# First units on x without its norm's factor, half units given out otherwise, bias in four transfers

## The reference

```python
h = _rms(x, norm1_g)                       # x / sqrt(mean(x*x) + eps) * gain
p_rwkv, q, k, v, qm, gates = split(h @ w_in)
o_a = _rwkv(p_rwkv, ...)                   # token recurrence of 8 heads x 64, delta rule, state S
o_b = sliding-window attention(q, k, v)    # 8 query / 2 key heads, ALiBi bias, sink, window 128
o_m = _mem_attend(qm, mk, mv)              # 4 heads x 128 over 256 memory tokens
br = stack([o_a, o_b, o_m]) @ w_branch     # each to 1024
x = x + sum(sigmoid(gates) * br) @ w_out
h = _rms(x, norm2_g)
a_in, u = split(h @ w_up)
x = x + (gelu(conv3(a_in)) * u) @ w_down
```

## Time and profile before

| what | us |
|---|---|
| median of 3 runs | 2136.68 |
| lowest, highest | 2133.88, 2139.18 |
| the profiled execution | 2136.24 |
| its span | 2134.2 |
| TensorE busy in it | 2066.6 |
| VectorE, ScalarE, GpSimd busy | 1264.5, 945.4, 148.0 |

### The profile page before, as it was taken

The page is one execution under the profiler, slowest core; times in us unless marked ns, Lnnn a source line. Parts: engine busy times, 40 slices in busy tenths (PEclk is TensorE's granted clock), DMA queues, the critical chain, the costliest instruction groups (busy, mean ns, idle before and its releaser), DMA issues.

```text
span 2134.2 us, 41128 instructions
## 1 busy us (share of the span) xinstructions
PE 2066.6 (97%) x17305; PEld 1965.7 (92%) x17305; DVE 1264.5 (59%) x2079; ACT 945.4 (44%) x1563; POOL 148.0 (7%) x238
## 2 busy tenths in 40 slices
PE   6999999999999999999999999999999999999999
PEld 5888899899999998889989999999878898899999
DVE  5566653656666545674446666654466645677753
ACT  5566332445444425643333544443375333455442
POOL 1000001001111000001000011100000110011110
PEclk9999999999999998999999999999999999999999
DMA  4422211354445452231124444445423213544544
GB/s 164 141 92 76 69 58 56 94 160 123 126 127 157 141 154 88 71 94 47 56 72 147 126 128 129 129 154 149 143 95 86 76 47 83 159 141 151 152 151 135
DMA packets 98487, 242.63 MB, mean 114 GB/s; under 512 B 24320, under 2 KB 38656, under 8 KB 98304
## 3 DMA queue, kind: packets, MB, share of 16 engines
q1 hardware_dynamic: 98304, 240.01, 37.3%
HBM read 233.88 MB, written 6.09 MB: 112 GB/s over the span
## 4 chain that ended last, share of the span: by engine, by line
PE 86%; DVE 6%; ACT 3%; issue 2%; DMA 1%; SPq 1%; DVEq 0%; ACTq 0%
PE sums L300 24%; PE sums L302 22%; PE sums L301 22%; PE px L1491 5%; DVE w_lo L476 1%; PE px L1504 1%; PE ps_t L1019 1%; PE ps_o L1041 1%; PE pz L1767 1%; PE ps_x L969 1%; PE ps_s L1005 1%; PE ps_o L1036 1%; ACT w_hi L318 1%; PE ps_s L1002 1%; DVE s L1120 1%
## 5 line engine op out<-in xcount | busy, mean ns | idle before, releaser
L300 PE MATMUL sums<-x_hi,w_hi 128*128 128x384 f32 (+1 forms) x2208 | 741.7, 336 | 22.2 <-DVE q L498 8.4
L302 PE MATMUL sums<-x_hi,w_lo 128*128 128x384 f32 (+1 forms) x2208 | 724.0, 328 | 0.0
L301 PE MATMUL sums<-x_lo,w_hi 128*128 128x384 f32 (+1 forms) x2208 | 723.8, 328 | 0.0
L476 DVE TENSOR_TENSOR w_lo<-raw,w_hi 128x1024 fp32r<-128x1024 f32 (+2 forms) x449 | 524.2, 1168 | 302.8 <-ACT w_hi L318 302.3
L318 ACT ACTIVATE w_hi<-raw 128x1024 fp32r<-128x1024 f32 (+1 forms) x452 | 441.0, 976 | 500.8 <-PE sums L302 279.5
L300 PEld LDWEIGHTS sums<-x_hi,w_hi 128*128 128x128 f32 x2208 | 417.7, 189 | 45.4 <-issue 29.8
L301 PEld LDWEIGHTS sums<-x_lo,w_hi 128*128 128x128 f32 x2208 | 418.4, 190 | 1.4
L302 PEld LDWEIGHTS sums<-x_hi,w_lo 128*128 128x128 f32 x2208 | 417.6, 189 | 0.0
L300 PE MATMUL sums<-h_hi,w_hi 128*128 128x384 f32 (+1 forms) x528 | 172.5, 327 | 0.0
L302 PE MATMUL sums<-h_hi,w_lo 128*128 128x384 f32 (+1 forms) x528 | 172.0, 326 | 0.0
L301 PE MATMUL sums<-h_lo,w_hi 128*128 128x384 f32 (+1 forms) x528 | 172.0, 326 | 0.0
(11 more groups left out here) (302 smaller groups left out, 2500.3 us busy)
## 6 DMA issues: line engine op xcount, KB each, us to landing
raw<-w_up SPq DMA_DIRECT2D x132, 512.0 KB, 3.6
raw<-w_gate SPq DMA_DIRECT2D x72, 512.0 KB, 3.6
raw<-w_down SPq DMA_DIRECT2D x48, 512.0 KB, 3.7
raw<-w_rwkv SPq DMA_DIRECT2D x42, 512.0 KB, 3.6
raw<-w_branch SPq DMA_DIRECT2D x72, 256.0 KB, 2.7
raw<-w_attn SPq DMA_DIRECT2D x30, 512.0 KB, 3.7
raw<-w_out SPq DMA_DIRECT2D x24, 512.0 KB, 3.6
raw<-w_down_end SPq DMA_DIRECT2D x24, 384.0 KB, 3.1
```

What stands on the lines that cost most here:

```text
L300: pe.matmul(out, wh[:, ws], n.hi[:, k, :], start=(n.begins and k == 0), stop=False)
L301: pe.matmul(out, wh[:, ws], n.lo[:, k, :], start=False, stop=False)
L302: mm = pe.matmul(out, wl[:, ws], n.hi[:, k, :], start=False, stop=(n.ends and k == n.kt - 1))
L476: dve.tensor_tensor(lo_of(c, u), raw_of(c, u), hi_of(c, u).bitcast(F32), ALU.subtract).then_inc(S["w_lo_dve"], 1)
```

## The change

Five edits, none of which adds or removes a matmul.

1. **Start.** Norm 0 is replaced by `first_*`, ten steps that hold units 0 and 1 among them (halves after each step: 0, 0, 1, 0, 2, 1, 0, 0, 0, 0, then one more). Units 0 and 1 (k and v of group 0) take `g_hi`, `g_lo`, the two parts of x times gain, and their sums are multiplied by the norm's factor `n1_y` when they are evacuated. Squares wait for x alone; `ones` is loaded behind the first part of x, `vecs` behind all of x. Unit 0 is split by VectorE, units 1 and 2 by GpSimd. The constants' loads and copies come behind unit 0's release of its weight tile. Norm 1 is woven with 12 halves instead of 14, and as `m_hi` lies on `g_hi`, it waits for units 0 and 1.
2. **Bias.** Four transfers of four heads each, two in the first step of `keys_sync` and two in the second, instead of eight of two heads in the first.
3. **Attention.** The 29 halves are 2, 2, 2 and then 23 spread over 20 steps. Before, they were spread over all 23.
4. **Recurrence.** The 48 halves have 3, 2 behind the preparation and then 26 over the rest of the scan; before 2 and then 29.
5. **Stores.** In the last group the tables are issued first, the state's stores three and four steps later.

```diff
-            unit("pa", g, m, T, a["w_attn"][m], DT, c.x_hi[:, :, x], c.x_lo[:, :, x],
-                 splitter="pool" if g == 0 and n < 3 else "dve", needs=ready if n == 0 else None)
+            if g == 0 and n < FIRST_UNITS:
+                unit("pa", g, m, T, a["w_attn"][m], DT, c.g_hi[:, :, x], c.g_lo[:, :, x],
+                     splitter="pool" if n else "dve", needs=gained if n == 0 else None)
+            else:
+                unit("pa", g, m, T, a["w_attn"][m], DT, c.x_hi[:, :, x], c.x_lo[:, :, x],
+                     splitter="pool" if g == 0 and n == 2 else "dve", needs=ready if n in (0, FIRST_UNITS) else None)
...
+        if n.kind == "pa" and m in (4, 5) and g == 0:
+            dve.wait_ge(S["n1_y"], ROOT)
+            dve.tensor_tensor((c.k_raw if m == 4 else c.vw)[:, 0:T], bank(c, n), c.n1_y[:, 0:T], ALU.mult).then_inc(free, 1)
...
+def first_act(act, c):
...
+    def rounded(k):
+        act.activation(c.g_hi[:, k, col], w.buf[:, k, :], ACT.Identity, scale=vec(c, w.gain, k)).then_inc(S["g_hi"], 1)
+
+    yield
+    for k in range(0, DT, 2):
+        act.wait_ge(S[f"x_in{k // 2}"], 16)
+        act.activation(c.first_sq[:, k, col], w.buf[:, k, :], ACT.Square).then_inc(S["even_sq"], 1)
+    yield
+    act.wait_ge(S["vecs_in"], 16)
+    for k in (0, 1):
+        rounded(k)
+    yield
+    for k in range(2, DT):
+        rounded(k)
+    yield
+    rsqrt_act(act, c, c.n1_xs[:, col], c.n1_t[:, col], c.n1_y[:, col], S["n1_y"], 1)
+    yield
+    for k in range(DT):
+        act.wait_ge(S["x_normed"], k + 1)
+        act.activation(w.hi[:, k, :], w.buf[:, k, :], ACT.Copy).then_inc(S["x_hi_done"], 1)
...
+def first_dve(dve, c):
...
+    def rest(k):
+        dve.wait_ge(S["g_hi"], k + 1)
+        dve.scalar_tensor_tensor(c.g_lo[:, k, col], w.buf[:, k, :], vec(c, w.gain, k), c.g_hi[:, k, col].bitcast(F32),
+                                 ALU.mult, ALU.subtract).then_inc(S["g_lo"], 1)
+
+    yield
+    for k in range(1, DT, 2):
+        dve.wait_ge(S[f"x_in{k // 2}"], 16)
+        dve.tensor_tensor(c.first_sq[:, k, col], w.buf[:, k, :], w.buf[:, k, :], ALU.mult).then_inc(S["odd_sq"], 1)
+    yield
+    dve.wait_ge(S["vecs_in"], 16)
+    for k in (0, 1):
+        rest(k)
+    yield
+    for k in (2, 3):
+        rest(k)
+    dve.wait_ge(S["n1_mean"], 1)
+    dve.tensor_scalar(c.n1_xs[:, col], c.ps_n[:, col], 1.0 / D, RMS_EPS, ALU.mult, ALU.add).then_inc(S["n1_y"], 1)
+    for k in range(4, DT):
+        rest(k)
+    yield
+    rsqrt_dve(dve, c.n1_xs[:, col], c.n1_t[:, col], c.n1_y[:, col], S["n1_y"], 1)
...
+    def bias(e):
+        for u in range(2):
+            sp.dma_start(c.bias[H[u], e, :, u * CHUNK:u * CHUNK + KEYS], c.a["alibi"][H[e], 2, :, :]).then_inc(S["bias_in"], 16)
...
-    for e in range(2):
-        for u in range(2):
-            for r in range(2):
-                sp.dma_start(c.bias[H[u], r, e, :, u * CHUNK:u * CHUNK + KEYS],
-                             c.a["alibi"][H[e], 2, 2 * r:2 * r + 2, :]).then_inc(S["bias_in"], 16)
-    yield
+    bias(0)
+    yield
+    bias(1)
...
-RECURRENCE_HALVES = PREP_STEPS * [1] + [2] + even(SCAN_STEPS - 1, 29) + [1, 1, 2, 1, 1, 1]
+ATTENTION_HALVES = [2, 2, 2] + even(ATT_STEPS - 3, 23)
+RECURRENCE_HALVES = PREP_STEPS * [1] + [3, 2] + even(SCAN_STEPS - 2, 26) + [1, 1, 2, 1, 1, 1]
...
-    norm = parts["norm"](0)
-    next(norm)
-    steps(parts["first"](), 1)
-    next(norm)
-    next(norm)
-    units(1)
-    steps(norm, NORM_STEPS - 3)
+    first = parts["first"]()
+    for n in (0, 0, 1, 0, 2, 1, 0, 0, 0, 0):
+        next(first)
+        units(n)
+    assert next(first, None) is None
+    units(1)
     steps(parts["start"](), 1)
     for g in range(len(GROUPS)):
         if g == 0:
-            units(2)
-            weave(parts["norm"](1), NORM_STEPS, 14)
+            weave(parts["norm"](1), NORM_STEPS, 12)
...
-        weave(parts["attention"](g), ATT_STEPS, 29)
+        beside(parts["attention"](g), ATTENTION_HALVES)
```

More of the change, by code:

```diff
@@ L585, in late @@
                               ALU.subtract).then_inc(S["h_lo"], 1)
+    split(0)
+    split(1)
     yield
@@ L675, in norm_pe @@
     yield from idle(3)
[L676 to L682, removed]
     pe.wait_ge(S["n1_added"], 7 * i)
@@ new lines, in first_pe, with first_pool @@
+def first_pe(pe, c):
+    S, w = c.S, norm_of(c, 0)
+    yield
+    pe.wait_ge(S["ones_in"], 16)
+    for k in range(DT):
+        pe.wait_ge(S["even_sq" if k % 2 == 0 else "odd_sq"], k // 2 + 1)
+        mm = pe.matmul(c.ps_n[:, 0:w.n], c.ones[:, :], c.first_sq[:, k, 0:w.n], start=(k == 0), stop=(k == DT - 1))
+    mm.then_inc(S["n1_mean"], 1)
+    yield from idle(FIRST_STEPS - 1)
+def first_pool(pool, c):
+    pool.wait_ge(c.S["vecs_in"], 16)
+    yield from idle(FIRST_STEPS)
+def first_dve(dve, c):
+    S, w = c.S, norm_of(c, 0)
+    col = slice(0, w.n)
+    def rest(k):
[6 more added lines that the diff above has]
+        dve.tensor_tensor(c.first_sq[:, k, col], w.buf[:, k, :], w.buf[:, k, :], ALU.mult).then_inc(S["odd_sq"], 1)
+    yield
+    dve.wait_ge(S["vecs_in"], 16)
+    for k in (0, 1):
+        rest(k)
+    yield
+    for k in (2, 3):
[4 more added lines that the diff above has]
+        rest(k)
+    yield
+    rsqrt_dve(dve, c.n1_xs[:, col], c.n1_t[:, col], c.n1_y[:, col], S["n1_y"], 1)
+    yield
+    dve.wait_ge(S["n1_y"], ROOT)
+    for k in range(DT + 2):
+        if k < DT:
+            dve.scalar_tensor_tensor(w.buf[:, k, :], w.buf[:, k, :], vec(c, w.gain, k), c.n1_y[:, col], ALU.mult,
+                                     ALU.mult).then_inc(S["x_normed"], 1)
+        if k >= 2:
+            dve.wait_ge(S["x_hi_done"], k - 1)
@@ L1879, in post_sync @@
     load_tables(sp, c, c.to_rows2, c.from_rows2)
-    yield from idle(POST_STEPS)
+    yield from idle(3)
+    if g == LAST:
+        for dst, src in (("o_rp", c.state[(N_CHUNKS - 1) % 2]), ("o_rs", c.state[N_CHUNKS % 2])):
+            for e in range(2):
+                sp.dma_start(c.a[dst][H[e], :, H[e]], src[H[e], :, :]).then_inc(S["stored"], 16)
+            yield
+    else:
+        yield from idle(2)
+    yield from idle(POST_STEPS - 5)
 def post_pe(pe, c, g):
@@ L2206, in allocate @@
     c.first_sq = c.ar[:, 14:22, :]
+    c.g_hi, c.g_lo = c.o_hi, c.o_lo
     c.q_sq, c.k_raw, c.k_sq = c.ar[:, 14:22, :], c.ar[:, 22, :], c.ar[:, 23, :]
@@ L2266, in _ @@
             in_order(dense_pe(pe, c), {
-                "first": lambda: first_wait(pe, c), "start": lambda: idle(1), "ready": lambda: start_wait(pe, c), "norm": of(pe, norm_pe), "memory": of(pe, memory_pe),
+                "first": lambda: first_pe(pe, c), "start": lambda: idle(1), "ready": lambda: start_wait(pe, c), "norm": of(pe, norm_pe), "memory": of(pe, memory_pe),
                 "keys": of(pe, keys_pe), "attention": of(pe, attention_pe),
@@ L2282, in _ @@
             in_order(dense_pool(pool, c), {
-                "first": lambda: first_wait(pool, c), "start": lambda: idle(1), "ready": lambda: start_wait(pool, c), "norm": nothing(NORM_STEPS), "memory": nothing(MEM_STEPS),
+                "first": lambda: first_pool(pool, c), "start": lambda: idle(1), "ready": lambda: start_wait(pool, c), "norm": nothing(NORM_STEPS), "memory": nothing(MEM_STEPS),
                 "keys": of(pool, keys_pool), "attention": nothing(ATT_STEPS),
```

68 lines of the change are left out of this document (30 added, 38 removed).

## The result

The changed kernel took 2146.49 us (median of 5 runs, 2144.07 to 2147.22), the kernel before beside it 2136.80 (5 runs, 2133.88 to 2139.18): a ratio of 1.0039, 95% interval 1.0027 to 1.0051. I had forecast 2133.0 with a range of 2120 to 2140. It is slower by 9.7 us. The profiled execution is the fastest of the five, 2144.07 with a span of 2142.3, so the traces explain 8 of the 9.7.

What follows compares the result with a forecast made beforehand. TensorE, busy 2066.6 of 2134.2 us, was taken as the bound. Start -3.4, bias -4.7, stores -2.1, attention +2.7, recurrence +3.9 sum to -3.6: 2132.6, plus 0.44 to the median, 2133.0; range 2120 to 2140.

Steps and rivals of the forecast that it cites:

- Bias and stores: Fewer bias transfers ahead of w_attn's load: -4.7 us; last group's tables issued before the state's stores: -2.1 us.
- The rival that the bias gives nothing: w_attn's slot in the ring is free only later, so no gain: 2137; chance 0.16 shared with Rival C.
- the contention term: Start: GpSimd's splits of units 1 and 2 slow VectorE beside them, +0.6 us within the start's -3.4.
- the 2 us that I had worked out for that rule: Start: by the shared port, VectorE's instructions beside a split stretch, making the start some 2 us worse than forecast.
- The hole ahead of unit 3: Start: TensorE idles 3.5 us before unit 3, which starts at 33.5 instead of 39.95.
- The pay-back: Start: waits of units 4 and 5 grow and take 1.5 to 3.2 us of unit 3's 6.4 us gain.
- Rival C: Start gives nothing: unit 3's six earlier us return as holes at units 3 to 5; 2136.5, chance 0.16 with its like.
- Attention: Halves moved ahead shorten the first turn's wait but lengthen the second's: 0, +0.4, +2.3 by group, +2.7 us in all.
- Recurrence: Scan's head even, later empty steps add waits: +1.3 us a group, +3.9 in all, bounds -4 and +7.
- rival B: Half-speed clock behind holes at unit 3, second turns of groups 1 and 2, three scan starts: +13.6, 2146.7; chance 0.10.
- Savings set against waits: Recurrence, per group: later empty steps cost 1.1 at k_n and 0.7 at xs; two fewer matmul changes save 0.2 each.

Runs made afterwards that it cites:

- The alone run: Attention's new list of halves alone, put into the kernel before: 2142.51 us, ratio 1.0025.
- the list alone: The recurrence's new list of halves alone, put into the kernel before: 2147.99 us, ratio 1.0056.
- The one experiment meant for that: The kernel before with the recurrence's new list, and one gate unit's w_lo ahead of the scan made by GpSimd instead of VectorE: 2145.20 us, ratio 1.0040.
- the two with GpSimd's split: One gate unit's w_lo by GpSimd, on the kernel before with the recurrence's new list (2145.20 us) and on that with bias and stores alone (2133.53 us).

## Why the prediction was wrong

**Bias and stores: right.** I had -4.7 and -2.1, the trace of the changed kernel shows -4.8 and -2.4, and the two together gave -9.5 (0.9942 to 0.9970) in the runs, which holds -6.8 at its edge. TensorE's waits for q fell from 2.37 and 2.33 to one of 1.82 in group 2 and from 1.52 to 0.34 in group 1. A part of what is over may lie in the tables' wait, for which I had 2.10 and no clock: in the four traces with the old order of the stores it is 2.10, 1.26, 3.16 and 2.37, the last two with a low stretch of 3.4 us behind them. The rival that the bias gives nothing is by its own terms -3.6 + 4.7 = +1.1, 2137.8 and not 2137. The section of the Trainium skill that I cited for a fixed cost of about 2 us a DMA ("DMA: Bandwidth & Descriptors", "Anatomy of one DMA — SWDGE (gpsimd) path") is on transfers that GpSimd issues. These are issued by SP, and eight issues in 5.17 us do not say when each transfer completes, so no run here tests that figure.

**Start: the contention term was too small; what the start is worth is open.** I had taken +0.6 for GpSimd's two splits beside VectorE. The root's last step alone took 2.07 more (2.63 for 0.56), and it stands on the path to unit 2, which started at 25.73 instead of my 23.6. The Trainium skill ("VectorE: DVE Perf Modes", section "Two Vector instructions with no wait between them") names the port that a Vector instruction with two SBUF inputs shares with GpSimd; the 2 us that I had worked out for that rule, and left out of my sum, was the right size. The hole ahead of unit 3, which I had put at 3.5, was 2.26, and unit 3 started at 35.03 instead of my 33.5. The pay-back came as I wrote, one unit later: waits of 1.29, 1.14 and 0.35 at units 5, 6 and 7, and a lead of 4.9 us at unit 3 that is 2.3 at unit 8. Rival C, that the start gives nothing, is neither shown nor excluded by the medians. The traces are against it: in the nine with the old start unit 8 begins at 62.9 to 64.3 us, in the two that have the changed kernel's start at 61.6 and 62.5, so some 1.6 us are gained there, and 1.5 of it is left at the start of attention.

**Attention: mechanism right, size too small.** I had +0.4 and +2.3 for groups 1 and 2, with waits of 0.5 and 1.7 at the first turn and 2.2 and 2.9 at the second. Measured were 0.32 and 1.12, 2.01 and 2.70. TensorE's idle time in the stage grew by 0.3, 1.1 and 2.0 us in the three groups, 3.4 in all where I had 2.7. Group 1's sum was wrong as it stood: its own terms, 0.5 + 2.2 - 2.40 and 0.8 for the values, give +1.1. What I had not seen is a late turn's wait of 0.43 in groups 0 and 1 and 0.82 in group 2. Beside that, in group 2 low stretches begin at 1567.3 and 1611.7, two of 1.7 us where there was one; but the second is not shown to be the list's, since the kernel with bias and stores alone has one at the same stage (1596.8) with the old list. The alone run's +6.5 against my +2.7 is within its bounds of +8.

**Recurrence: the term that failed.** I had +3.9 with an upper bound of +7; it is +12.0. Three steps of the term were wrong.

- *The clock.* I counted one wait of 2.3 for w_lo as equal to the two of 1.01 and 1.37 that it replaces. In groups 0 and 1 it measured 2.14 and 2.13, as priced, but each was followed by 3.4 us at half speed, 1.7 us, where the two short ones had been followed by none. I had this in rival B with a chance of 0.10 and left it out of the term and of its bound.
- *Group 2.* I read the head of group 0 and took it three times. In group 2 the kernel before has one wait of 1.32 there, behind that for merged, and the changed kernel 2.54 and 0.31: +1.5 where I had 0 (the list alone, with the low stretch ahead of its wait, 1.41 and 0.31). There the clock adds nothing, since a low stretch stood there before.
- *Savings set against waits.* k_n I had at +1.1 (measured 1.03, in group 2 1.37) and the xs step at +0.7 (0.95: the program waits there for VectorE's last product of the inverse, which ends just before; the profile calls it "issue"). From these I took 0.4 for fewer changes between dense and small matmuls; about 0.2 of it is seen, as what is left of +3.6 when idle time and clock are taken off.

The wait of the kernel before at the head of group 2:

```profile
1668.08 2.02 PE L1491 MATMUL px<-m 64*64 64x64 f32 x62 [1.32 <-DVE m L1692]
```

The idle time grew by 2.1, 2.0 and 3.8 us in the three groups instead of 1.3 each, 7.9 in all, and the clock adds 3.4.

B forecast 2146.7, the median is 2146.5, and that they agree is mostly luck. B makes the whole loss out of clock, 13.6 us. Low stretches did come at the start, at the scans and at group 2's second turn, as it says, but several of them replace stretches that the kernel before had, and without any the two lists would still have lost some 11 us of idle time (7.9 in the recurrence, 3.4 in attention).

Does the wait itself bring the low clock? The one experiment meant for that moved the wait and did not take it away. But all thirteen kernels of this case have the same small matmuls at the scan's head. In groups 0 and 1, four kernels (the changed one, the list alone, the two with GpSimd's split) have a wait of 2.13 to 2.76 us there, and in all eight places a low stretch begins in the wait or within 1.4 us of its end. In the other nine kernels no wait there is over 1.37, and none of the eighteen places has one; this is the window of the kernel before, at full clock:

```profile
236.00:240.00 4.00, 2.21 (x86) 1.00 0.24 70
```

So at this place it is the wait and not the small matmuls. Over all traces, behind the start, 38 of 52 waits of 2.1 to 3.3 us have a low stretch that begins in the wait or within 1.5 us of its end, and none of 221 waits of 0.8 to 1.7 us. It is no fixed rule: the same wait of 3.04 to 3.07 at group 2's first turn has a low stretch behind it in three traces and none in seven. Here is one of the seven, in the kernel with bias and stores, right behind its wait of 3.06, beside the window behind its 2.40:

```profile
1543.60:1547.00 3.40, 3.40 (x25) 1.00 0.02 5
832.20:835.60 3.40, 3.40 (x15) 0.50 0.00 0
```

So such a wait costs 1.7 us more in most places, not in all, and for the same wait not in every execution. What decides it stays open.

## What to carry to other kernels

Where TensorE is 97% busy and every engine's program is one fixed order, moving work ahead of one wait hands the wait to the next step: count what stands behind in VectorE's queue, and take the sum over the whole stage, not over the wait that is seen. Price one long wait above two short ones of the same sum, since the clock may fall behind it (behind 38 of 52 waits of 2.1 to 3.3 us here, 1.7 us each). Read a stage in every group before you multiply: the waits of one group need not stand in the next. GpSimd is no relief for VectorE when it takes over a split and VectorE has work beside it: 2.38 us of it cost VectorE 1.93, the split itself 1.2.

## What the hardware showed beyond that

GpSimd's split nearly stops the VectorE instruction beside it: 0.56 became 2.63, 1.76 became 3.69. It is not only those with two inputs from SBUF: the copy of a 64x64 block, with one, took 2.36 beside GpSimd's split in the kernel before and 0.14 in the changed kernel, where GpSimd was idle. GpSimd's own 2.4 us did not grow. Its memset did no such harm: beside one of 1.81 us at 34.48 in the changed kernel, VectorE's sum of 128x256 took its usual 0.41.

Two executions can differ by 1 to 3 us at the same matmul in stretches that their programs share, with idle times that agree to 0.02 us: the stretches at 0.5 begin at other places and last 3.4, 6.8 or 10.3 us. A difference of 2 us between two profiles is no evidence, and between two medians of this case, whose intervals are some 3 us to either side, it is not told either.
